# Two of eight token tiles through a dense pass over all experts, with weights scatter-added in DRAM, in a one-core hybrid-mixer and PEER kernel

## What is computed

```
s = einsum('thpc,pnc->thpn', q, sub_keys); sv, si = top_k(s, 16)
fv, fi = top_k(sums of both halves, 16);   g = softmax(fv)
act = gelu(einsum('td,thkd->thk', xt, expert_u[eidx]))
out = einsum('thk,thkd->td', g * act, expert_v[eidx])
```

## Time and profile before

| | us |
|---|---|
| Median of 3 runs (lowest, highest) | 3465.17 (3459.03, 3474.46) |
| Span of the profiled execution | 3457.6 |
| Median less this span | 7.6 |
| Busy: PE, DVE, ACT, POOL | 2170.6, 2140.8, 648.4, 1980.4 |
| Mean granted TensorE clock, share of 2.4 GHz | 0.766 |
| Bytes moved by DMA | 1160.93 MB, mean 336 GB/s |

### The profile page before, as it was taken

One profiled execution on the slowest core, in us unless ns is written; L12 is line 12 of the kernel. 1 busy time (PEld: TensorE's weight loads), 2 busy tenths in 40 slices (PEclk: granted clock), 3 DMA queues, 4 the chain that ended last, 5 costly groups with the idle time before them and its releaser, 6 DMA issues.

```text
span 3457.6 us, 32843 instructions
## 1 busy us (share of the span) xinstructions
PE 2170.6 (63%) x10776; PEld 1129.7 (33%) x10776; DVE 2140.8 (62%) x5482; ACT 648.4 (19%) x1393; POOL 1980.4 (57%) x2079
## 2 busy tenths in 40 slices
PE   7999999646654567555654567456763677444433
PEld 6888644223221232123221333123321343111110
DVE  5652665567666666657675666666765766665563
ACT  2221232112211121102210222103310232100000
POOL 0000366776666666666566656666666556666665
PEclk9999999867776677767876778767885787666656
DMA  6103799999999999999999899999999989999998
GB/s 233 46 24 129 257 350 363 390 369 366 355 385 375 366 370 358 387 365 358 349 389 371 338 361 341 389 362 367 366 396 368 343 322 359 365 368 368 369 370 320
DMA packets 335778, 1160.93 MB, mean 336 GB/s; under 512 B 36916, under 2 KB 41720, under 8 KB 335608
## 3 DMA queue, kind: packets, MB, share of 16 engines
q0 software_dynamic: 294912, 1073.87, 81.9%
q1 hardware_dynamic: 40696, 84.95, 6.8%
HBM read 1140.83 MB, written 17.84 MB: 335 GB/s over the span
## 4 chain that ended last, share of the span: by engine, by line
PE 27%; issue 19%; POOL 18%; another core or an unknown queue 14%; DVE 12%; DMA 6%; ACT 3%; SPq 0%; DVEq 0%; POOLq 0%; ACTq 0%
POOL work L914 9%; POOL work L898 9%; PE xs L1728 8%; PE xs_ahead L1728 8%; PE acc L1728 6%; DVE work L1602 5%; PE bank L1728 5%; DMA work<-expert_u,chosen 3%; DMA work<-expert_v,idx_v 2%; DVE work L1256 1%; DMA weights<-w_out 1%; DVE work L1248 1%; ACT L1142 1%; DVE rest L1501 0%
## 5 line engine op out<-in xcount | busy, mean ns | idle before, releaser
L898 POOL DMA_INDIRECT work<-expert_u,chosen x1024 | 984.9, 962 | 736.3 <-DVE chosen L1256 347.1
L914 POOL DMA_INDIRECT work<-expert_v,idx_v x1024 | 990.5, 967 | 725.5 <-remote 299.1
L1602 DVE CUSTOM_DVE_ANT_0 work<-work,xs 128x1024 f32<-128x1024 f32 x875 | 1053.9, 1218 | 395.3 <-DMA work<-expert_u,chosen 240.8
L1728 PE MATMUL acc<-work,lw 128*32 128x512 f32 x4096 | 772.1, 823 | 610.9 <-DMA work<-expert_v,idx_v 449.6
L1728 PEld LDWEIGHTS acc<-work,lw 128*32 128x32 f32 x4096 | 143.7, 134 | 1060.8 <-issue 544.6
L1728 PE MATMUL bank<-weights,n2T 128*128 128x256 f32 x1024 | 262.4, 410 | 10.4 <-issue 10.1
L1728 PEld LDWEIGHTS bank<-weights,n2T 128*128 128x128 f32 x1024 | 205.1, 206 | 123.6 <-issue 95.6
L1602 DVE CUSTOM_DVE_ANT_0 work<-work 128x1024 f32<-128x1024 f32 x128 | 156.2, 1227 | 112.8 <-DMA work<-expert_u,chosen 100.3
L1728 PE MATMUL xs_ahead<-work,neg_tri 128*128 128x512 f32 (+1 forms) x176 | 136.2, 867 | 135.7 <-issue 59.5
L1728 PE MATMUL xs<-work,weights 128*128 128x128 f32 x1472 | 176.5, 282 | 0.0
L2029 PE MATMUL bank<-ident,w_spread 128*128 128x128 f32 x64 | 25.5, 398 | 237.3 <-ACT idx_v L933 154.7
(11 more groups left out here) (232 smaller groups left out, 2541.1 us busy)
## 6 DMA issues: line engine op xcount, KB each, us to landing
work<-kv_dram SPq DMA_DIRECT2D x72, 256.0 KB
work<-expert_u,chosen POOLq DMA_INDIRECT x1024
work<-expert_v,idx_v POOLq DMA_INDIRECT x1024
weights<-w_in SPq DMA_DIRECT2D x6, 2048.0 KB, 19.3
mix_dram<-work SPq DMA_DIRECT2D x34, 256.0 KB, 2.4
weights<-w_out SPq DMA_DIRECT2D x4, 2048.0 KB
weights<-w_queryT SPq DMA_DIRECT2D x4, 2048.0 KB, 12.4
kv_dram<-work SPq DMA_DIRECT2D x18, 256.0 KB, 2.5
```

What stands on the lines that cost most here:

```text
L898: pool.indirect_dma_start(out=ring[:, s, :], out_offset=None, in_=expert_u, in_offset=bass.IndirectOffsetOnAxis(ap=chosen[:, G % KEPT_HEAD ...
L914: pool.indirect_dma_start(out=ring[:, s, :], out_offset=None, in_=expert_v, in_offset=bass.IndirectOffsetOnAxis(ap=idx_v[:, G % PH, col:co ...
L1602: nc.vector.tensor_tensor_reduce(ring[:, row, :], ring[:, row, :], rows, 1.0, 0.0, ALU.mult, ALU.add, dots[:, d:d + 1]).then_inc(dotted, 1)
L1728: return nc.tensor.matmul(out_, lhsT, rhs, start=start, stop=stop, skip_group_check=True)
```

## The change

Tiles 4 and 6 no longer gather. Their heads are scored and picked as before, but the gate of each pick is added by an indirect DMA to a table in DRAM, `w_dram`, of 16384 experts by 256 tokens, which is set to zero in the front. Then all 16384 experts are run over the 256 tokens of both tiles in 128 steps of 128 experts: PE multiplies a block of `expert_u` (handed over by the host a second time, rearranged as `u_blocks`) by the tokens, ACT applies gelu, DVE multiplies by the block of the table, PE multiplies by the block of `expert_v` and sums in PSUM. The steps stand at slots 536 to 758, beside the gathers of the last two gathering tiles. Six tiles gather, so the stream has 768 slots. The mixings start every 64 slots (67 once) at shorter steps, and the last ends at slot 507; the rows that the dots need, and `h`, go through DRAM. The rings are 6 rows for `u` and 8 for `v`, and 10 and 16 at the end, in the space of the scoring weights. Cut to its core:

```diff
-RING_U = 7
-RING_V = 10
-HEADS = LAST * PH
+PASSES = [1, 2, 3, 5, 7, 8]
+DENSE = [4, 6]
+GT = len(PASSES)
+RING = 16
+EXTRA = 12
+HEADS = GT * PH
+ROUTED = LAST * PH
...
+PERIODS = {1: 8, 2: 8, 3: 8, 4: 7, 5: 6, 6: 5, 7: 5, 8: 5}
+MIX_EACH = 64
+MIX_AT = {2: 14, 3: 112}
+for _M in range(3, TILES):
+    MIX_AT[_M + 1] = MIX_AT[_M] + max(MIX_EACH, FAST_STEPS["blocks"] + (_M + 1) * PERIODS[_M] + FAST_TAIL["rows"])
...
+D_STEPS = N_BLOCKS = 128
+DENSE_AT = 536
+DENSE_LAG = 2
+DENSE_SLOTS = 224
+D_U, D_V, D_W, D_G, W_EACH = 4, 4, 2, 3, 4
...
-V_RINGS = [(0, [8, 9, 10, 11, 12, 15, 16]), (63, [7, 8, 9, 10, 11, 12, 15,16]),           (79, [13, 7, 8, 9, 10, 11, 12, 15, 16]), (133, [14, 13, 7, 8, 9, 10, 11, 12, 15, 16])]
-U_RINGS = [(0, [0, 1, 2, 3]), (36, [4, 0, 1, 2, 3]), (61, [5, 4, 0, 1, 2, 3]), (73, [6, 5, 4, 0, 1, 2, 3])]
+V_RINGS = [(0, [8, 9, 10, 11, 14, 15]), (55, [6, 8, 9, 10, 11, 14, 15]), (63, [7, 6, 8, 9, 10, 11, 14, 15]),
+           (560, [16, 17, 18, 19, 20, 21, 22, 23, 7, 6, 8, 9, 10, 11, 14, 15])]
+U_RINGS = [(0, [0, 1, 2, 3]), (36, [4, 0, 1, 2, 3]), (61, [5, 4, 0, 1, 2, 3]), (570, [24, 25, 26, 27, 5, 4, 0, 1, 2, 3])]
...
+def dense_at(j):
+    return DENSE_AT + j * DENSE_SLOTS // D_STEPS
...
+def scatters_at(s):
+    found = []
+    for d in range(len(DENSE) * PH):
+        r = (DENSE[d // PH] - 1) * PH + d % PH
+        first = scores_at((DENSE[d // PH] - 1) * PH) + 26 + TOPK * (d % PH)
+        if first <= s < first + TOPK:
+            found.append((d, r, s - first))
+    return found
...
+            def zero_w(c):
+                n = N_BLOCKS * D_TOKENS // ZEROS
+                sp.dma_start(w_rows[:, c * n:(c + 1) * n].rearrange("i (r n) -> i r n", n=P * 4),
+                             lw[:, :].unsqueeze(1).broadcast_to([P, n // (P * 4), P * 4])).then_inc(w_zeroed, 16)
...
+            def load_u_d(j):
+                wait(sp, z_d_done, j - D_U + 1)
+                sp.dma_start(u_d[j % D_U], u_blocks[j]).then_inc(first_u_in[j % D_U], 16)
+            def load_v_d(j):
+                wait(sp, out_d_done, j - D_V + 1)
+                sp.dma_start(v_d[j % D_V], expert_v.rearrange("(i j) d -> i j d", j=N_BLOCKS)[:, j, :]).then_inc(
+                    first_v_in[j % D_V], 16)
...
+            def scatter(d, k):
+                if k == 0:
+                    if d == 0:
+                        pool.wait_ge(w_zeroed, 16 * ZEROS)
+                    pool.wait_ge(cell_ready, d + 1)
+                    pool.wait_ge(gate_d_ready, d + 1)
+                    wait(pool, scattered, 16 * TOPK * d)
+                pool.indirect_dma_start(out=w_cells, out_offset=bass.IndirectOffsetOnAxis(
+                                            ap=cell[:, d % PH, k:k + 1], axis=0),
+                                        in_=gate_d[:, d % PH, k:k + 1], in_offset=None, compute_op=ALU.add
+                                        ).then_inc(scattered, 16)
...
+                for d, _, c in scatters_at(s):
+                    scatter(d, c)
                 if G < HEADS:
                     gather_u(G, k)
                 if G > 0:
                     gather_v(G - 1, k)
...
+            def gelu_d(j):
+                act.wait_ge(z_d_done, j + 1)
+                wait(act, out_d_done, j - D_G + 1)
+                nc.scalar.activation(g_d[j % D_G], bank[6][:, 0:D_TOKENS], ACT.Gelu).then_inc(
...
+            def mult_d(j):
+                g = j // W_EACH
+                dve.wait_ge(gelu_d_ready, j + 1)
+                dve.wait_ge(first_w_in[g % D_W], 16 * (g // D_W + 2))
+                TT(g_d[j % D_G], g_d[j % D_G], w_d[g % D_W][:, j % W_EACH, :], ALU.mult).then_inc(g_d_ready, 1)
...
+            def dense_z(j):
+                if j == 0:
+                    pe.wait_ge(first_n2T_in, 16 * (1 + len(DENSE)))
+                    pe.wait_ge(gain_copied, 1)
+                    pe.wait_ge(y_ready, 3)
+                pe.wait_ge(first_u_in[j % D_U], 16 * (j // D_U + 2))
+                wait(pe, gelu_d_ready, j)
+                for k in range(KC):
+                    last = mm(bank[6][:, 0:D_TOKENS], u_d[j % D_U][:, k, :],
+                              n2T_d[:, k, :, :].rearrange("p a t -> p (a t)"), k == 0, k == KC - 1)
+                last.then_inc(z_d_done, 1)
+            def dense_out(j):
+                pe.wait_ge(g_d_ready, j + 1)
+                pe.wait_ge(first_v_in[j % D_V], 16 * (j // D_V + 2))
+                for a in range(len(DENSE)):
+                    for n in range(2):
+                        last = mm((xs, xs_ahead)[a][:, n, :], g_d[j % D_G][:, a * P:(a + 1) * P],
+                                  v_d[j % D_V][:, n * 512:(n + 1) * 512], j == 0, j == D_STEPS - 1)
+                last.then_inc(out_d_done, 1)
```

More of the change, by code:

```diff
@@ L370, in program @@
         tri = take(P)
+        W36 = TILES * MH
+        gate_rows_sb = [take(P)[0:MH, :] for _ in range(6)]
+        lf, tmp4, f_cols = take(MH), take(MH), take(MH)
+        m_row = take(TILES + 1)[0:MH, :]
+        dec_row = take(TILES)[0:MH, :]
+        dec_blk = take(MH)[0:MH, :]
         assert cut[0] <= 4 * D
@@ new lines, in _ @@
+                for q in range(2, GT + 1):
+                    T = PASSES[q - 1]
+                    if s == max((q - 2) * SLOTS + 2, MIX_AT[T] + tail(T, "rows") + 3):
+                        load_rows(q)
+                    if s == (q - 1) * SLOTS + OUT_AT + 2:
+                        store_y(q - 1)
+                        load_pass_h(q)
+                if s == MIX_AT[LAST] + tail(LAST, "rows") + 3:
+                    begin_dense()
+                    load_dense_h(0)
+                if s == DENSE_AT - 1:
+                    for g in range(D_W):
+                        load_w_d(g)
@@ new lines, in _ @@
+                for j in dense_steps(s):
+                    if j + D_U < D_STEPS:
+                        load_u_d(j + D_U)
+                    if 0 <= j - DENSE_LAG and j - DENSE_LAG + D_V < D_STEPS:
+                        load_v_d(j - DENSE_LAG + D_V)
+                    if j % W_EACH == W_EACH - 1 and j // W_EACH + D_W < D_STEPS // W_EACH:
+                        load_w_d(j // W_EACH + D_W)
+                if s == dense_at(D_STEPS - 1) + 1:
+                    load_dense_h(1)
+            for f in range(GT, TILES):
+                store_y(f)
@@ L1119, in copy_n2T @@
                 wait(act, scores_done, PH * (T - 1))
+                wait(act, n2T_stored, 16 * sum(1 for t in DENSE if t < T))
                 for k in range(KC):
@@ L1193, in mixing @@
                     copy_n2T(M)
+                if n == tail(M, "rows") and 1 < M and M in PASSES:
+                    copy_rows(M)
             for kind, what in ITEMS:
@@ L1699, in _ @@
                     invert(0)
-            for T in range(0, LAST + 2):
+            for T in range(0, GT + 2):
                 for n in range(0 if T else SLOTS + FIRST_SLOT, slots(T)):
@@ L2073, in mixing @@
                     n2_t(M)
+                if n == tail(M, "rows") and 1 < M and M in PASSES:
+                    n2_rows_ahead(M)
             square_sums(0)
```

740 lines of the change are left out of this document (438 added, 302 removed).

## The result

The kernel with the change takes 3612.26 us (median of 4, 3605.81 to 3623.96); the kernel before took 3462.59 beside it (4 runs, 3459.03 to 3474.46). The ratio is 1.040, with a 95% interval of 1.035 to 1.045. The forecast was 3386 us, with a range up to 3560. The profiled execution has a span of 3604.1 us.

A forecast was written before the change was run, and what follows sets the result against it. The prediction took the DMA engines to bound the kernel, with POOL a close second. Its terms, 353 + 369 + 510 + 986 + 33 + 1064 + 23 + 40, gave 3378 us, 3386 with 7.6 added for the median; 80% range 3210 to 3560.

The forecast's parts named there:

- Slots 269 to 524, 256 at 3.85 us: Stretch with scatters: POOL's three indirect DMAs a slot, each at a gather's price, 3.74 us, plus imperfect meshing; 986 us.
- dear scatters: Rival, chance 0.18: scatters in slots 269 to 524 cost more; upper end 4.67 a slot, middle 1196 us, total 3596.
- dense pass: Slots 536 to 759: PE sets the pace, DMA right behind; 1038 us plus 26 of mutual waiting, 4.75 a slot, 1064 us.
- The scatters' load on the DMA engines: Slots 269 to 524: a scatter takes the DMA engines 0.5 us, 1.1 with reading and writing; upper end 1.4.
- The 16 waits for landing: Slots 269 to 524: POOL waits 16 times for the previous head's scatters to land, 1 or 2 us each.
- the +24 us at the end: Slots 760 to 767 at 2.9 us, 23 us, then 40 us as before from the last `gather_u`: 63 us forecast.
- Slots 0 to 111: First stretch of the stream: 369 us after 359, +10 for the smaller `v` ring, bounds 0 and +20.
- The bytes: Whole kernel: net -86 MB of 1161, 7%; about 235 us shorter if bytes at 370 GB/s were all.
- Slots 112 to 268: Mixing and scoring twice as dense, smaller `v` ring: 157 slots at 3.25 us, 510 us; ends 2.99 and 3.6.
- Crowded mixing: Rival, chance 0.08: steps waiting for each other stretch slots 112 to 268 to 3.8, 269 to 524 to 4.1; 3536 us.
- Slow strided rows: Rival, chance 0.10: dense pass's `expert_v` rows come at half of 413 GB/s, DMA needs 1097 us; +73, total 3459.
- Cheap scatters: Rival, chance 0.14: POOL hands over a scatter in 0.6 us; slots 269 to 524 at 3.1, 190 us less, 3196.

The follow-up runs named there:

- run 2: Changed kernel with scatters that overwrite instead of adding, on chip 15: 3429.06 us, 1.073 of the kernel before.
- run 4: Changed kernel with overwriting scatters and the dots of slots 128 to 479 reading PSUM, on chip 0: 3335.83 us, 1.043 of the kernel before.
- run 3: Changed kernel with the dots of slots 128 to 479 reading an operand from PSUM instead of SBUF, on chip 15: 3492.49 us, 1.094 of the kernel before.
- Run 9: Kernel before with rings cut to 6 and 8 rows, chip 2: 3501.18 us, ratio 1.008; with all dots from SBUF too: 3507.96 us, 1.011.
- run 10: Both kernels unedited, profiled on chip 15: kernel before 3198.59 us; changed kernel 3607.74 us against 3196.14, ratio 1.128.
- run 1: Changed kernel without the scatters and the waits for them: 3162.69 us on chip 15 (0.990 of the kernel before), 3159.30 on chip 0 (0.988), 3206.47 on chip 2 (0.929).
- run 7: Changed kernel reading neighbouring rows of `expert_v` in each dense step instead of rows 512 KB apart, on chip 0: 3614.44 us.
- run 6: Changed kernel leaving out two of the four output products of every dense step, all loads kept, on chip 15: 3538.43 us.
- run 5: Changed kernel with every second scatter left out, on chip 0: 3314.22 us, 1.037 of the kernel before.

## Why the prediction was wrong

**The step that failed** is "Slots 269 to 524, 256 at 3.85 us". Its mechanism was right: POOL takes a third indirect DMA in each slot and sets the pace, with the DMA share down at 0.79. Its price was not. The term was 3 x 1.245, about 3.72 in rounded figures (3 x 0.94 + 0.90), and 0.13 for meshing; measured it is 3.72, +0.70 for the scatter-add (1.64 instead of 0.94, runs 2 and 4), +0.46 for gathers of 1.26 and 1.08 (run 3 takes 0.40 of it away), +0.08 of waits for landing: 4.96. That is 1.11 us over the term, 284 us in all, where 0.31 was enough to end the gain.

The **dear scatters** were the rival that came true, beyond their upper end. Two reads and a write had been priced at twice a gather's 0.94, 4.67 a slot; the scatter stayed under that (1.64 against 1.88), and the gathers, which I took as fixed, went over it. That the rival's total of 3596 us stands so near the measured 3612 is luck: its middle was 74 us too short and the dense pass 86 us too long. The rows to see this were there: the earlier trace rows averages gathers over all tiles, but tile 1, whose dots read `rows1` in SBUF, had gathers of 1086 and 1088 ns between 400 and 700 us of the trace of before, and the tiles with the rows in PSUM 948 and 951. The views, from 400 to 700 us and from 800 to 3000 us:

```profile
L914 POOL DMA_INDIRECT work<-expert_v,idx_v x90 | 98.0, 1088 | 66.5 <-PE acc L1728 40.4 <-issue 23.6 <-remote 2.5
L898 POOL DMA_INDIRECT work<-expert_u,chosen x90 | 97.7, 1086 | 38.3 <-issue 27.0 <-DVE dots L1602 11.3
```

```profile
L914 POOL DMA_INDIRECT work<-expert_v,idx_v x737 | 701.1, 951 | 533.5 <-remote 247.3 <-issue 187.8 <-PE acc L1728 94.3
L898 POOL DMA_INDIRECT work<-expert_u,chosen x736 | 697.7, 948 | 268.8 <-issue 210.2 <-DVE dots L1602 58.6
```

The change puts all rows in SBUF, which I read in the code as a detour through DRAM, and never as a change of DVE's operands. The Trainium skill, SBUF — State Buffer, under "Who interferes with whom", says that a DVE instruction with two SBUF inputs contends with a GpSimd instruction that reads SBUF. Run 3 agrees, with 0.40 us a slot, if issuing an indirect DMA counts as such an instruction (its indices lie in SBUF; what POOL reads is in no trace). Run 9 adds that it costs next to nothing while POOL has time to spare.

**The scatters' load on the DMA engines** was put at 0.5 to 1.1 us. An estimate from the shares on chip 15 agrees: 0.78 of 5.01 us with the scatters (run 10) less 0.95 of 3.29 without (run 1) is 0.8 us a slot. It set no pace, since the DMA share of the stretch stayed at 0.79. The 16 waits for landing, put at 1 or 2 us each, came to 19.6.

**Dense pass, 1064 forecast, 978 measured.** PE sets the pace at full clock and the DMA engines stand right behind, as said. The 26 us of mutual waiting did not come (974.62 of 979 busy), and a step is a little shorter than the 7.03 us of the earlier trace rows, since the next instruction starts before the record of the last one ends. PE's instructions in order, one step and the start of the next:

```profile
3001.60 3.62 PE L2038 MATMUL bank<-weights 128*128 128x256 f32 x16
3005.06 1.88 PE L2038 MATMUL xs<-work 128*128 128x512 f32 x4
3006.77 1.88 PE L2038 MATMUL xs_ahead<-work 128*128 128x512 f32 x4
3008.49 3.62 PE L2038 MATMUL bank<-weights 128*128 128x256 f32 x16
```

6.89 us from step to step, 18 us less over 128. The remaining 42 us are not saved but come later. The first dense product on PE starts at 2549.86 us and the last ends at 3571, 1021 us against the 1038 of the forecast's sum:

```profile
2549.86 4.75 PE L2038 MATMUL bank<-weights 128*128 128x256 f32 x16
...
3569.14 1.88 PE L2038 MATMUL xs_ahead<-work 128*128 128x512 f32 x4
```

The gathers of slots 536 to 759 lie between 2538 and 3517 us: with rings of 10 and 16 rows POOL runs ahead, and six first products and eight second ones still stand before PE when slot 760's gather starts. That fits the +24 us at the end. The term's size was right to 2%, and its place by slots was not.

**Slots 0 to 111** took 22 us more than before, not 10. Run 9 gives 24 for the small rings alone, so their bounds (0 and +20) were a little short. **The bytes** came out as forecast: 1075.32 MB after 1160.93, 86 less. **Slots 112 to 268**: 3.22 against 3.25. **Crowded mixing** was wrong: without the scatters 269 to 524 run at 3.29 to 3.47 us (run 1). **Slow strided rows** were wrong: the dense pass ran at 389 GB/s and took 979 us, where the rival's DMA engines alone needed 1097, and run 7. The rule of the Trainium skill, DMA: Bandwidth & Descriptors, under latency and other measured facts, that copies with a pitch of 512 KB reach 207 GB/s, does not show in these rows of 4 KB that arrive beside gathers. **Cheap scatters** was wrong by the sign of its difference.

**What was not seen at all** is the chip. The forecast took its gain from a trace of a kernel that the DMA engines bound at 364 GB/s. Without its scatters the change would gain 7% there, 248 us, and 1.3% or less where they give 404, 35 to 41 us (run 1). The scatters cost 434 us on chip 2 and 445 on chip 15 (3607.74 less 3162.69), more than either.

**No version beat both kernels.** Dots from PSUM in slots 128 to 479 take 115 us off the change on chip 15 (3607.74 less 3492.49), and if as much came off 3614 on chip 2, it would still be above the kernel before. With the add dropped too, 3336 us is under the 3460 of chip 2 (not run there) but over the 3199 of its own chip, loses a weight where two heads pick the same expert, and reads the wrong token rows for its dots. The DMA engines behind PE leave the dense pass little: run 6 with a quarter of the columns gone is worth 57 us there. Not tried: scatters spread over more slots, several tiles' weights in fewer scatters, or a table made by other means than an indirect DMA.

## What to carry to other kernels

When a queue is near its limit, price each new instruction on it by an operation of the same kind, and if the trace has none, let the break-even point and not the likeliest price decide. Ask also what the change does to the instructions that are already there: an operand moved from PSUM to SBUF on DVE made POOL's gathers 14 to 28% longer in the mean, which was nearly free while POOL had slack and cost 0.40 us in each slot once it had none. A mean that rises can be two populations: count the instructions that start beside the suspected neighbour and those that don't. And a gain in bytes is worth what the chip at hand makes of it: look at the rate on more than one chip.

## What the runs showed of the hardware that was not expected

- A scatter-add of 128 elements of 4 bytes takes POOL 1.63 to 1.65 us in the mean, a plain scatter 1.01 to 1.10, a gather of 128 rows of 4 KB 0.94 and up, each with 0.30 us to the next. The bytes don't matter to POOL; the add does.
- An indirect DMA issued while a dot with both operands in SBUF is running is held up, one issued just before the dot is not: `gather_u` 1.70 against 0.98 us in the change, scatters 2.09 against 1.68 in run 5, which is why they take 1.91 us in the mean there.
- The same kernel moves 404 GB/s on one chip and 366 on another in the same stretch, with times of 3199 and 3460 us. That the memory and not the DMA engines makes the difference is not shown; both are full in either profile, at shares of 1.02 and 0.97.
